# A gated two-branch decoder layer: two RMS-type norms by full-row sums and Newton roots instead of diagonal broadcasts

## The reference

```python
h = rmsnorm(x, ln_pre[i])
z = h @ w_in[i]
(c_val, c_glu, c_gate, q, k, v, a_gate, g_conv, g_attn) = split_columns(z)
ya = conformer_conv(c_val, c_glu, w_dw[i], b_dw[i], conv_ln_g[i], conv_ln_b[i], w_pw[i])
ya = (ya * jax.nn.silu(c_gate)) @ w_br_conv[i]
yb = sliding_window_sink_attention(q, k, v, sinks[i], positions)
yb = (yb * jax.nn.silu(a_gate)) @ w_br_attn[i]
m = jax.nn.sigmoid(g_conv) * ya + jax.nn.sigmoid(g_attn) * yb
x = x + rmsnorm(m @ w_out[i], ln_post[i])
x = x + jax.nn.sigmoid(x @ w_ple_gate[i]) * (p[i] @ w_ple_proj[i])
```

## Time and profile before

| | |
|---|---|
| median of 3 runs | 1170.94 us (1170.62 to 1171.06) |
| the profiled execution | 1170.57 us |
| its span, first to last instruction | 1168.8 us |
| busy: TensorE / VectorE / ScalarE / GpSimd | 1162.1 / 840.0 / 377.5 / 18.2 us |
| mean granted TensorE clock | 0.999 of full speed |
| chain that ended last | TensorE 96%, VectorE 2%, DMA 1%, ScalarE 1% |

### The profile page before, as it was taken

One profiled execution on the slowest core, in us unless ns is written; L12 is line 12 of the kernel. 1 busy time (PEld: TensorE's weight loads), 2 busy tenths in 40 slices (PEclk: granted clock), 3 DMA queues, 4 the chain that ended last, 5 costly groups with the idle time before them and its releaser, 6 DMA issues.

```text
span 1168.8 us, 16097 instructions
## 1 busy us (share of the span) xinstructions
PE 1162.1 (99%) x6304; PEld 947.2 (81%) x6304; DVE 840.0 (72%) x944; ACT 377.5 (32%) x670; POOL 18.2 (2%) x17
## 2 busy tenths in 40 slices
PE   9999999999999999999999999999999999999998
PEld 8888888888888888877777888888888888888886
DVE  6999999999999984699886775673333445357665
ACT  6331221221221121366665432431112112444431
POOL 1020000000000000000000000000000000000000
PEclk9999999999999999999999999999999999999999
DMA  9622122222222323211212111333233232334655
GB/s 353 271 90 72 58 86 72 65 79 72 72 72 72 99 54 86 54 56 56 73 56 74 36 54 38 108 106 105 75 108 107 73 108 94 121 117 140 211 162 179
DMA packets 35530, 116.40 MB, mean 100 GB/s; under 512 B 4480, under 2 KB 4992, under 8 KB 35488
## 3 DMA queue, kind: packets, MB, share of 16 engines
q1 hardware_dynamic: 25120, 82.29, 22.3%
q10 hardware_dynamic: 10368, 33.56, 8.6%
HBM read 92.10 MB, written 20.97 MB: 97 GB/s over the span
## 4 chain that ended last, share of the span: by engine, by line
PE 96%; DVE 2%; DMA 1%; ACT 1%; issue 0%; SPq 0%; POOL 0%; ACTq 0%; DVEq 0%; POOLq 0%
PE psg L457 81%; PE psg L733 6%; PE psg L477 2%; PE psb L647 1%; PE psg L704 1%; DMA conv<-xT 1%; PE psg L665 1%; ACT probs L968 1%; PE psg L699 1%; PE psg L506 1%; PE psb L569 0%; PE psg L551 0%; DVE smax L1398 0%; PE psb L530 0%; DVE probs L1422 0%
## 5 line engine op out<-in xcount | busy, mean ns | idle before, releaser
L457 PE MATMUL psg<-h_hi,w_hi 128*128 128x512 f32 x768 | 237.0, 390 | 0.0
L457 PE MATMUL psg<-h_hi,w_lo 128*128 128x512 f32 x768 | 236.5, 389 | 0.0
L457 PE MATMUL psg<-h_lo,w_hi 128*128 128x512 f32 x768 | 236.4, 389 | 0.0
L824 ACT ACTIVATE w_hi<-w_raw 128x1024 fp32r<-128x1024 f32 x112 | 118.5, 1058 | 225.3 <-PE psg L457 210.4
L1164 DVE TENSOR_TENSOR w_lo<-w_raw,w_hi 128x1024 fp32r<-128x1024 f32 x114 | 139.4, 1223 | 69.3 <-ACT w_hi L824 69.0
L457 PEld LDWEIGHTS psg<-h_hi,w_lo 128*128 128x128 f32 x768 | 144.1, 188 | 30.1
L457 PEld LDWEIGHTS psg<-h_lo,w_hi 128*128 128x128 f32 x768 | 144.1, 188 | 30.0
L457 PEld LDWEIGHTS psg<-h_hi,w_hi 128*128 128x128 f32 x768 | 143.8, 188 | 30.4 <-issue 0.8
L1317 DVE SCALAR_TENSOR_TENSOR conv<-u,cols,conv 128x1024 f32<-128x1024 f32 x120 | 154.2, 1285 | 0.0
L1317 DVE SCALAR_TENSOR_TENSOR work<-u,cols,work 128x1024 f32<-128x1024 f32 x112 | 145.6, 1300 | 0.0
L733 PE MATMUL psg<-h_hi,w_hi 128*128 128x512 f32 x128 | 51.8, 405 | 0.0
(11 more groups left out here) (229 smaller groups left out, 1733.8 us busy)
## 6 DMA issues: line engine op xcount, KB each, us to landing
w_raw<-weights SPq DMA_DIRECT2D x114, 512.0 KB, 3.5
gates<-ring ACTq DMA_DIRECT2D x24, 512.0 KB, 2.7
ring<-gates ACTq DMA_DIRECT2D x24, 512.0 KB, 3.6
x_rows<-x_rows SPq DMA_DIRECT2D x8, 512.0 KB, 9.9
conv<-xT SPq DMA_DIRECT2D x8, 512.0 KB, 14.1
ple<-ple_out SPq DMA_DIRECT2D x8, 512.0 KB, 13.3
x_ring<-xT ACTq DMA_DIRECT2D x16, 256.0 KB, 3.5
ple_all<-ple ACTq DMA_DIRECT2D x8, 512.0 KB, 4.2
```

The source lines that it names most:

```text
L457: mm = nc.tensor.matmul(psg[:, slot, h * HALF:(h + 1) * HALF], w[:, wslot, (wk + k) * P:(wk + k + 1) * P], r[:, k, h * HALF:(h + 1) * HALF ...
L824: nc.scalar.activation(w_hi[:, j % 2, :], w_raw[:, j % 2, :], ACT.Copy).then_inc(w_hi_ready, 1)
```

## The change

The mean squares, the roots on GpSimd and the diagonals of the two later norms are removed. VectorE splits `sums` itself into a high part and a low part (`sums_in_parts`, the low part in place), and TensorE multiplies both by the full 128 x 128 ones (`wide_sums`), so that each partition holds the sum of each token. VectorE then makes the inverse roots on whole rows: mean plus epsilon, a first guess by arithmetic on the bits of the number, and three Newton steps of three operations each, of which each waits for the one before. For the layer norm the sums are split ahead of m=4 of the stage from D0 on, `wide_sums` stands at k=1 of D0+6, guess and first step ahead of m=6, the other two steps ahead of m=7, and the rows end in `sums`, which `norm_scale` now reads. For the post norm `wide_sums` stands at k=1 of H1+1 and I0+1; guess and first step follow `tile_low` at m=0, the other two steps follow it at m=1. The columns of `x1_beside` move: none in the first two tiles, then one, two, two, one, one, one. In the stage from H1 on, `x1_full` and its followers now come behind `add_square` and `tile_low` of the same m, except for the last column, which comes ahead of them; ScalarE has the same order.

```diff
         def x1_beside(m):
-            return ((), (0, 1), (2,), (3,), (4,), (5,), (6,), (7,))[m]
+            return ((), (), (0,), (1, 2), (3, 4), (5,), (6,), (7,))[m]
...
             def norm_pair(first, rhs_hi, rhs_lo, ready, half, h):
...
+                def square_sums(k):
                     if k == 1:
-                        broadcast((h + 4,), (h,), diag_hi, diag_hi[:, NB // 2:])
-
-                tile(first // 2, 0, rhs_hi, rhs_lo, ready, (half,), sum_squares)
-                tile(first // 2, 1, rhs_hi, rhs_lo, None, (half,), roots)
-
-            def mean_square(ready, count, blocks=range(NB), bank=2):
-
-                pe.wait_ge(ready, count)
-                for c in blocks:
-                    mm = nc.tensor.matmul(psb[:, bank, c:c + 1], sums[:, c * P:(c + 1) * P], ones[:, 0:1].bitcast(F32),
-                                          start=True, stop=True)
-                mm.then_inc(msq_done, 1)
+                        wide_sums(2 + h, (h,), post_hi[:], sums_lo[:, h * HALF:(h + 1) * HALF])
+
+                tile(first // 2, 0, rhs_hi, rhs_lo, ready, (half,))
+                tile(first // 2, 1, rhs_hi, rhs_lo, None, (half,), square_sums)
+
+            def wide_sums(count, banks, hi, lo):
+
+                pe.wait_ge(parts_ready, count)
+                for part, source in enumerate((hi, lo)):
+                    for n, bank in enumerate(banks):
+                        mm = nc.tensor.matmul(psb[:, bank, :], ones[:], source[:, n * HALF:(n + 1) * HALF],
+                                              start=(part == 0), stop=(part == 1))
+                mm.then_inc(bcast_done, 1)
...
-            tile(D0 // 2 + 3, 0, h_hi, h_lo, beside=lambda k: mean_square(var_summed, KT + 1) if k == 1 else None)
-            tile(D0 // 2 + 3, 1, h_hi, h_lo, beside=lambda k: broadcast((3, 3), hi=diag_ln_hi, lo=diag_ln_lo) if k == 1 else None)
+            tile(D0 // 2 + 3, 0, h_hi, h_lo,
+                 beside=lambda k: wide_sums(1, (0, 1), var_hi[:], sums_lo[:]) if k == 1 else None)
+            tile(D0 // 2 + 3, 1, h_hi, h_lo)
...
-            rsqrt(3)
-            rsqrt(4, slice(0, NB // 2))
-            rsqrt(5, slice(NB // 2, NB))
...
-            act.wait_ge(bcast_done, 2)
+            act.wait_ge(ln_root, 1)
...
             for m in range(KT):
+                if m < KT - 1:
+                    w_out_tile((H0 + KT + m) // 2, m % 2, m, 1)
                 for k in x1_beside(m):
                     x1_high(0, k)
-                w_out_tile((H0 + KT + m) // 2, m % 2, m, 1)
+            w_out_tile((H0 + 2 * KT - 1) // 2, (KT - 1) % 2, KT - 1, 1)
...
+            def sums_in_parts(hi, part):
+
+                own.step(nc.vector.tensor_copy(hi, sums[:, part]))
+                own.wait()
+                nc.vector.tensor_tensor(sums_lo[:, part], sums[:, part], hi.bitcast(F32), ALU.subtract).then_inc(parts_ready, 1)
+
+            def root_step(part, guess, step):
+
+                own.step(nc.vector.tensor_tensor(step, guess, guess, ALU.mult))
+                own.wait()
+                own.step(stt(step, step, -0.5, sums[:, part], ALU.mult, ALU.mult))
+                own.wait()
+                own.step(stt(guess, step, 1.5, guess, ALU.add, ALU.mult))
+                own.wait()
+
+            def start_root(count, source, part, guess, step):
+
+                dve.wait_ge(bcast_done, count)
+                own.step(nc.vector.tensor_scalar(sums[:, part], source, 1.0 / D, EPS, ALU.mult, ALU.add))
+                own.wait()
+                own.step(nc.vector.tensor_scalar(guess.bitcast(I32), sums[:, part].bitcast(I32), -0.5, ROOT_SEED,
+                                                 ALU.mult, ALU.add))
+                own.wait()
+                root_step(part, guess, step)
...
+                if m == 4:
+                    dve.wait_ge(var_summed, KT + 1)
+                    sums_in_parts(var_hi[:], slice(0, S))
                 if m == 6:
-                    variance(3)
-                    diagonal(3, hi=diag_ln_hi, lo=diag_ln_lo)
+                    start_root(2, banks01, slice(0, S), ring[:, 0, :], ring[:, 1, :])
+                if m == 7:
+                    root_step(slice(0, S), ring[:, 0, :], ring[:, 1, :])
...
+                    stt(sums[:], ring[:, 1, :], 1.5, ring[:, 0, :], ALU.add, ALU.mult).then_inc(ln_root, 1)
...
-                nc.vector.tensor_tensor(conv[:, k, :], conv[:, k, :], banks01, ALU.mult).then_inc(ln_scaled, 1)
+                nc.vector.tensor_tensor(conv[:, k, :], conv[:, k, :], sums[:], ALU.mult).then_inc(ln_scaled, 1)
...
-                own.step(stt(wout[:, k, half], wout[:, k, half], col("ln_post", k), psb[:, h, :], ALU.mult, ALU.mult))
+                own.step(stt(wout[:, k, half], wout[:, k, half], col("ln_post", k), guess, ALU.mult, ALU.mult))
...
+            def post_root(h, m):
+
+                half = slice(h * HALF, (h + 1) * HALF)
+                if m == 0:
+                    start_root(3 + h, psb[:, h, :], half, guess, step)
+                if m == 1:
+                    root_step(half, guess, step)
+                    root_step(half, guess, step)
+
+            def post_sums(h):
+
+                dve.wait_ge(sq_used, (h + 1) * KT)
+                sums_in_parts(post_hi[:], slice(h * HALF, (h + 1) * HALF))
...
             for m in range(KT):
                 if m == 0:
-                    variance(4, slice(0, NB // 2))
-                    diagonal(4, slice(0, NB // 2), lo=diag_hi[:, NB // 2:])
-                some_x1(0, m)
+                    post_sums(0)
+                if m == KT - 1:
+                    some_x1(0, m)
                 add_square((H0 + KT + m) // 2, m % 2, m, 1)
                 tile_low(H0 + KT + m + 2)
+                post_root(0, m)
+                if m < KT - 1:
+                    some_x1(0, m)
             for m in range(KT):
                 if m == 0:
-                    variance(5, slice(NB // 2, NB))
-                    diagonal(5, slice(NB // 2, NB), lo=diag_hi[:, NB // 2:])
+                    post_sums(1)
                 some_x1(1, m)
                 tile_low(I0 + m + 2)
+                post_root(1, m)
```

More of the change, by code:

```diff
@@ L43 @@
 MAGIC = 12582912.0
+ROOT_SEED = 1597463007.0
 TWO_PI = (6.28125, 0.0019350051879882812, 3.0199159819567e-07)
@@ L202, in build @@
         var_summed = sem("var_summed")
-        msq_done = sem("msq_done")
+        parts_ready = sem("parts_ready")
+        ln_root = sem("ln_root")
         msq_ready = sem("msq_ready")
@@ L1173, in split_low @@
                 stt(dst[:, k, :], src, scale, hi[:, k, :].bitcast(F32), ALU.mult, ALU.subtract).then_inc(lo_ready, 1)
-            def variance(n, c=slice(0, NB)):
-                dve.wait_ge(msq_done, n - 2)
-                nc.vector.tensor_scalar(mean_sq[:, c], psb[:, 2, c], 1.0 / D, EPS, ALU.mult, ALU.add).then_inc(msq_ready, 1)
+            def sums_in_parts(hi, part):
[17 more added lines that the diff above has]
+                root_step(part, guess, step)
             def variance_of_rows(c):
@@ L1511, in _ @@
                 a2, j = (D0 + m) // 2, m % 2
+                if m == 4:
+                    dve.wait_ge(var_summed, KT + 1)
+                    sums_in_parts(var_hi[:], slice(0, S))
                 if m == 6:
-                    variance(3)
-                    diagonal(3, hi=diag_ln_hi, lo=diag_ln_lo)
+                    start_root(2, banks01, slice(0, S), ring[:, 0, :], ring[:, 1, :])
+                if m == 7:
+                    root_step(slice(0, S), ring[:, 0, :], ring[:, 1, :])
+                    own.step(nc.vector.tensor_tensor(ring[:, 1, :], ring[:, 0, :], ring[:, 0, :], ALU.mult))
+                    own.wait()
+                    own.step(stt(ring[:, 1, :], ring[:, 1, :], -0.5, sums[:], ALU.mult, ALU.mult))
+                    own.wait()
+                    stt(sums[:], ring[:, 1, :], 1.5, ring[:, 0, :], ALU.add, ALU.mult).then_inc(ln_root, 1)
                 dve.wait_ge(tanh_ready, m + (2 * KT + 1))
@@ L1597, in x1_full @@
                 nc.vector.tensor_tensor(wout[:, k, half], wout[:, k, half], x_ring[:, k % 4, :], ALU.add).then_inc(full_ready, 1)
+            guess, step = tanh_t[:, 0:HALF], tanh_t[:, HALF:]
+            def post_root(h, m):
[8 more added lines that the diff above has]
+                sums_in_parts(post_hi[:], slice(h * HALF, (h + 1) * HALF))
             def x1_low(h, k):
```

12 lines of the change are left out of this document (3 added, 9 removed).

## The result

The changed kernel takes 1175.43 us (median of 6 runs, 1174.27 to 1176.62); the kernel before, beside it, 1171.00 (1170.62 to 1171.13). The ratio is 1.0038, 95% interval 1.0027 to 1.0049: slower by 4.4 us.

What follows compares the result with a forecast made beforehand. TensorE, busy 1162.1 of 1168.8 us, was taken to bound the kernel. -3.76 + 0.25 + 3.84 + 2.78 = +3.1 us gave 1174.1 for the median; own range 1173.0 to 1175.4, wider 1171.2 to 1175.8.

Steps and rivals of the forecast that it cites:

- the last rival: More is lost than counted: integer operation and cast at two-tensor rate, each round slightly longer; 1175.5 and over, chance 0.10.
- What the change takes from TensorE: -3.76: Mean squares of both norms: 16 plain fp32 products (32 records) leave TensorE, saving 3.76 us.
- Layer norm: 0.25: At k=7 of E0 TensorE waits for the last o_lo, losing about 0.25 us, between 0 and 0.6.
- The unknown prices: VectorE's cast and integer guess, without rows of their size: one-tensor rate chosen; the two-tensor rate would add 0.3 us each.
- the rival of chained steps without a gap: VectorE's chained operations step as closely as free ones, shrinking the waits: 1172.8 us, chance 0.08.
- First half: 1.11, 0.57, 1.78: Post norm: TensorE stalls of 1.11 us before H1+7, 0.57 at k=7 of I0, 1.78 before I0+1.
- The parts of the sums: 0.38: In I0+1 TensorE asks for the second half's sum parts before VectorE has them: stall of 0.38 us.
- Second half: 1.42, 0.68, 0.68: Post norm: TensorE stalls 1.42 us before I0+4, then 0.68 for each of two rounds of column pairs, to I0+6.
- a clock that drops behind a gap: Sign that would make the forecast wrong, for TensorE, whose clock was granted in full before; no size given.

Runs made afterwards that it cites:

- experiment 7: The change with the x1 columns' high and low parts made one tile later in both halves of the post norm: 1167.41 us, ratio 0.9970.
- experiment 3: The change with the last two Newton steps of the post norm's second half moved from m=1 to m=0: 1173.15 us, ratio 1.0018.
- experiments 1: The kernel before with only the layer norm's part of the change: 1169.37 us, ratio 0.9987.
- experiments 2: The change in the post norm only, with the layer norm as in the kernel before: 1176.38 us, ratio 1.0047.
- experiment 4: The change with the last two Newton steps of the post norm left out in both halves: 1171.02 us, ratio 1.0003.
- in 9: The kernel of experiment 7 with unused chained maxima on VectorE ahead of the weight split of I0+1: 1171.59 us.
- experiment 5: The change plus second half's last two steps at m=0, and in the first half low parts after the next weight split, H1+7 read out earlier, columns moved: 1174.94 us.
- experiment 6: The change with high and low parts of x1 columns one tile later in first half: 1170.96; with the second half's last two Newton steps at m=0 too: 1169.63.
- experiment 8: Kernel before, unused chained maxima on VectorE ahead of I1 weight splits: at three tiles 1179.74, 1180.04; only I1+2, eight 1172.81, ten 1175.92 to 1178.69.

## Why the prediction was right, and where its sum was off

The forecast was 1174.1 and slower; 1175.43 was measured. That is inside the range given last, 1171.2 to 1175.8, but at the edge of the forecast's own, 1173.0 to 1175.4. The upper end of the wider range was there for the last rival, slower operations and rounds, which did not come; the clock, which had no term, took that room. So the waits were foreseen as they came, and that the time stayed in the range is in part luck. In the order of the prediction:

- *What the change takes from TensorE: -3.76.* From H0+2 on 1.92 less in the run without waits (experiment 7), where 1.91 was counted. Up to H0+2 the changed kernel is 1.33 earlier (996.63 against 997.96): -1.85, +0.26 for the layer norm, and 0.26 more before D0+6, where the change has no part. Right.
- *Layer norm: 0.25.* It cost 0.26. VectorE reached each point within 0.33 us of the count: the five operations from 708.40 to 714.13 (713.93 counted), the gate product of m=7 at 727.70 (727.37), the end of the last o_lo at 733.60 (733.27).

VectorE in order of time after the change, tile D0+6 and on, answering to the earlier trace rows:

```profile
708.40 1.22 DVE L1190 TENSOR_SCALAR sums<-psb 128x1024 f32<-128x1024 f32 x1
709.66 0.69 DVE L1192 TENSOR_SCALAR ring<-sums 128x1024 int32<-128x1024 int32 x1
710.38 1.23 DVE L1180 TENSOR_TENSOR ring<-ring 128x1024 f32<-128x1024 f32 x1
711.64 1.22 DVE L1182 SCALAR_TENSOR_TENSOR ring<-ring,sums 128x1024 f32<-128x1024 f32 x1
712.90 1.23 DVE L1184 SCALAR_TENSOR_TENSOR ring<-ring 128x1024 f32<-128x1024 f32 x1
...
727.70 1.21 DVE L1542 SCALAR_TENSOR_TENSOR work<-tanh_t,psg 128x1024 f32<-128x1024 f32 x1
...
732.37 1.23 DVE L1170 SCALAR_TENSOR_TENSOR o_lo<-qo,o_hi 128x1024 fp32r<-128x1024 f32 x1 [1.19 <-ACT o_hi L830]
```

- *The unknown prices.* The integer guess took 0.69 for 1024 elements and the cast 0.42 for 512, the low end that was chosen. Chained steps of 1024 went at 1.26 (710.38 to 711.64), 0.12 over the free 1.14, and of 512 at 0.72 to 0.73. So the rival of chained steps without a gap falls. The Trainium skill ("VectorE: DVE Perf Modes", "The DRAIN you can't avoid") holds that a semaphore behind each operation costs nothing extra, measured there on copies; for the two-tensor operations of this trace, at 1.26 against 1.14, it does not hold.
- *First half: 1.11, 0.57, 1.78.* By idle and 0.26 they came to 1.08, 0.56 and 1.74. A round with one column took 5.23 (1050.30 to 1055.53), one with two 6.62, where 5.23 and 6.61 were counted. VectorE in order of time after the change, a round of two columns and the first of the next, answering to the earlier trace rows, and ahead of it the sums' parts, the guess and the round of one column:

```profile
1032.95 0.42 DVE L1174 CAST post_hi<-sums 128x512 fp32r<-128x512 f32 x1
...
1039.02 0.43 DVE L1192 TENSOR_SCALAR tanh_t<-sums 128x512 int32<-128x512 int32 x1
1039.48 0.69 DVE L1180 TENSOR_TENSOR tanh_t<-tanh_t 128x512 f32<-128x512 f32 x1
1040.21 0.69 DVE L1182 SCALAR_TENSOR_TENSOR tanh_t<-tanh_t,sums 128x512 f32<-128x512 f32 x1
...
1050.30 0.74 DVE L1619 SCALAR_TENSOR_TENSOR wout<-wout,cols,tanh_t 128x512 f32<-128x512 f32 x1
...
1055.53 0.74 DVE L1619 SCALAR_TENSOR_TENSOR wout<-wout,cols,tanh_t 128x512 f32<-128x512 f32 x1
...
1062.15 0.74 DVE L1619 SCALAR_TENSOR_TENSOR wout<-wout,cols,tanh_t 128x512 f32<-128x512 f32 x1
```

- *The parts of the sums: 0.38.* In the profiled execution no such wait came: with the matmuls at half speed the wide sums asked later and found the parts there. In experiment 3, where the clock stayed full, it came and cost 0.36. So the term was right, and the clock hid it.
- *Second half: 1.42, 0.68, 0.68.* It came to 1.53, 0.59 and 0.73. The halves act apart: from H0+2 on, the run with waits in the second alone takes 166.99, 2.98 more than the run with none (2.78 counted), the one with waits in the first alone 168.02, 4.01 more (3.84 counted).
- *What was missed: the clock.* The prediction named a clock that drops behind a gap among what would make it wrong, but gave it no term. In the profiled execution it cost 1.60 and hid the 0.38: 1.22 over the sum. The rest of 5.2 against 3.1 is 0.15 from the restarts (with the few matmuls behind it each costs 0.12 to 0.14, where 0.10 was counted), 0.26 before D0+6, and 0.45 of the end: from the start of the last matmul 4.9 us before, and in experiments 1, 2, 4, 7 and 9, but 5.3 to 5.4 after, and in 3, 5 and 6, so that it does not go with the change.

How much of the 4.4 us between the medians is the clock's can be told less surely. The executions after the change lie at 1174.27 and 1174.42, and from 1175.07 to 1176.62. The profiled one, with the fall, is of the upper ones; without the 1.22 that the fall cost it would be at 1174.6, near the lower two and the forecast. In three experiments the profiled execution lies as its clock says: in 3, without a fall, 1172.27 among 1171.84 to 1173.79; in 4, with one, 1171.77, above the six at 1170.68 to 1171.02; in 9, with one, above the three at the bottom. Of an execution without a profile the record has the mean granted clock, to three digits. No profiled execution without a fall has less than 0.999, but a fall as short as the one after, or in 2, 4 and 9, prints 0.999 too. In 3 the five slowest executions (1173.37 to 1173.79) have 0.997 or 0.998 and the six others 0.999 or 1.000; in 9 the four slowest (1171.80 to 1172.49) have 0.998 and the others 0.999 or 1.000. A mean of 0.997 is at least 5.9 us at the lower level, more than the 5.4 behind the last matmul, so part of that lies ahead of it. So the fall comes in some executions of the same kernel and not in others; how many have a short one can't be told.

What decides whether the clock falls stays open. At I0+1 a wait of 1.48 or 1.49 brought the fall in three profiles (after, experiments 2 and 4) and not in one (3); waits of 1.57 and 1.63 in I1 did not bring it, nor those of 1.41 (H1+7) and 1.38 (k=7 of I0) in experiment 5; 2.32, 2.82 and 3.58 did. The length alone does not tell the cases near 1.5 apart.

## What to carry to other kernels

When work is put on an engine with free time, draw the ring of hand-overs that it joins and compare one round of it with the tile time of the engine that bounds the kernel: VectorE was 74% busy and still made TensorE wait, because a round of two columns took 6.6 us against 5.44. The cure was not less work but a lag of one tile, so that each engine takes up what the other finished a tile ago. Moving one piece only put the waits elsewhere: the low parts behind the split made the round longer (experiment 5), and the early steps brought two other waits (experiment 6). And a wait of TensorE near 1.5 us or longer may cost more than its length, as it did here in some executions: give the clock a term of its own in the range.

## What the runs showed of the hardware that was not expected

- Behind a wait TensorE ran at its lower clock (granted 0.50) although it was fully fed: for 3.5 us behind 1.48 (a cost of 1.60) and for 6 behind 2.82 (1134.29 to 1140.3). The fall came with the first matmul (after), 0.6 us later (experiment 4) or 0.9 us ahead of it, within the wait (experiment 8, ten maxima).
- A cast to fp32r took 0.42 us and an integer operation with constants 0.43 for 512 elements, where a two-tensor operation takes 0.69.
